# Norms, scaling and gate rows one stage ahead, joins pipelined by token half, shifted norms written in full first

## The reference

```
x = x + 0.5 * swiglu(rmsnorm(x, ffn1_norm[i]), ...)
h = rmsnorm(x, mix_norm[i]);  x = x + mixer(h)       # deltanet, stick-breaking, sparse attention, deltanet
x = x + 0.5 * swiglu(rmsnorm(x, ffn2_norm[i]), ...)
```

```
m = split(silu(c) @ mod_w + mod_b, 9)       # shift, scale, gate for three places
modulate(x, g, shift, scale) = rmsnorm(x, g) * (1 + scale) + shift
x = x + 0.5 * gate * swiglu(modulate(x, ...))
```

## Time and profile before

| | us |
|---|---|
| median of 3 runs | 3886.77 (3882.24 to 3892.0) |
| the profiled execution's own time | 3886.8 |
| its span, first to last instruction | 3885.0 |
| PE busy | 3564.5 (92%) |
| DVE busy | 2276.5 (59%) |
| ACT busy | 1839.1 (47%) |
| POOL busy | 606.9 (16%) |

### The profile page before, as it was taken

How to read it: one execution, slowest core, us unless ns; L and a number is a source line. 1 busy time by engine, 2 the same in 40 slices (tenths; PEclk the granted TensorE clock), 3 DMA queues, 4 the chain that set the end, 5 groups by cost and what they waited for, 6 DMA issues and landing times. The chain is left out here.

```text
span 3885.0 us, 45081 instructions
## 1 busy us (share of the span) xinstructions
PE 3564.5 (92%) x18342; PEld 2997.1 (77%) x18342; DVE 2276.5 (59%) x2608; ACT 1839.1 (47%) x2400; POOL 606.9 (16%) x208
## 2 busy tenths in 40 slices
PE   7998799999899996899998799899998789999999
PEld 6887677788778876688887688787878568787887
DVE  4475458776566667656666454555555554555654
ACT  4453257665356562456554244444443344444443
POOL 0001129572042320142400200000000000000000
PEclk9998899999999998899998899999999899999999
DMA  5542046665276752376743035454544115354453
GB/s 217 188 148 87 1 174 239 225 240 204 101 271 233 275 206 106 134 258 238 265 166 131 1 109 189 153 189 149 198 163 164 62 68 194 142 200 157 152 195 136
DMA packets 89978, 653.57 MB, mean 168 GB/s; under 512 B 10032, under 2 KB 10032, under 8 KB 10928
## 3 DMA queue, kind: packets, MB, share of 16 engines
q1 hardware_dynamic: 78768, 573.10, 40.4%
q0 software_dynamic: 11008, 77.60, 5.6%
HBM read 649.61 MB, written 1.05 MB: 167 GB/s over the span
## 5 line engine op out<-in xcount | busy, mean ns | idle before, releaser
L1424 DVE TENSOR_TENSOR w_lo<-raw,w_hi 128x2048 fp32r<-128x2048 f32 x540 | 1421.0, 2636 | 661.0 <-ACT w_hi L1003 660.7
L1003 ACT ACTIVATE w_hi<-raw 128x2048 fp32r<-128x2048 f32 x540 | 1031.0, 1913 | 601.2 <-PE acc L518 410.2
L516 PE MATMUL wrk<-w_hi,h_hi 128*128 128x512 f32 (+1 forms) x2496 | 973.3, 390 | 61.5 <-DVE w_lo L1424 41.4
L518 PE MATMUL wrk<-w_hi,h_lo 128*128 128x512 f32 (+1 forms) x2496 | 956.2, 383 | 0.0
L517 PE MATMUL wrk<-w_lo,h_hi 128*128 128x512 f32 (+1 forms) x2496 | 955.1, 383 | 0.0
L516 PEld LDWEIGHTS wrk<-w_hi,h_hi 128*128 128x128 f32 x2496 | 473.7, 190 | 157.8 <-DVE w_lo L1424 52.3
L2082 POOL TENSOR_TENSOR arena<-arena,c 128x2048 f32<-128x2048 f32 x92 | 492.1, 5356 | 473.1 <-ACT arena L1003 447.1
L518 PEld LDWEIGHTS wrk<-w_hi,h_lo 128*128 128x128 f32 x2496 | 472.9, 189 | 93.3
L517 PEld LDWEIGHTS wrk<-w_lo,h_hi 128*128 128x128 f32 x2496 | 474.0, 190 | 85.2 <-issue 0.2
L516 PE MATMUL acc<-w_hi,hid_hi 128*128 128x512 f32 x1144 | 447.9, 392 | 9.4 <-DVE hid_lo L1507 9.4
L518 PE MATMUL acc<-w_hi,hid_lo 128*128 128x512 f32 x1144 | 445.9, 390 | 0.0
(11 more groups left out here) (254 smaller groups left out, 3501.4 us busy)
## 6 DMA issues: line engine op xcount, KB each, us to landing
raw<-in_wts SPq DMA_DIRECT2D x540, 1024.0 KB, 4.8
arena<-in_mods POOLq DMA_DIRECT2D x72, 1024.0 KB, 5.2
const<-in_const SPq DMA_DIRECT2D x1, 2176.0 KB, 10.1
c<-in_bias POOLq DMA_DIRECT2D x8, 256.0 KB, 3.4
x<-in_x SPq DMA_DIRECT2D x1, 1024.0 KB, 5.3
c<-in_c SPq DMA_DIRECT2D x1, 1024.0 KB, 4.8
out<-x SPq DMA_DIRECT2D x1, 1024.0 KB, 3.9
row<-in_rows SPq DMA_DIRECT2D x1, 512.0 KB, 11.5
```

Of the source, the lines that this page charges most:

```text
L516: nc.tensor.matmul(o, l_h, r_h, start=first, stop=False, skip_group_check=True)
L518: return nc.tensor.matmul(o, l_l, r_h, start=False, stop=last, skip_group_check=True)
L1003: return nc.scalar.activation(o, i, f, **kw)
L1424: tt(w_lo[:, ns % SLOTS, :], raw[:, ns % SLOTS, :], w_hi[:, ns % SLOTS, :].bitcast(F32), ALU.subtract).then_inc(lo_ready, 1)
```

## The change

`mod` and `final_norm` no longer stand between stages: the silu rows are made in step 1 of ffn2_0, `mod` in step 2 of ffn2_3, the final norm in step 2 of b0_ctx (`INSIDE`). The statistics and the normalise of b0_ctx, b0_ffn0 and b0_attn's context are made in step 4 of the operation before (`AHEAD`), and c is loaded at the start of ffn2_3. `follower` now names the next operation whatever it is. `opens` has three kinds: "ready" (normalised ahead), "late" (as before) and "norm". Ahead of ready and late ones the last FFN turns t=0 between its last downs. Ahead of norm ones the t=0 downs of the last step come before the t=1 downs of the step before it, statistics and normalise of t=0 are done before the last product, and t=0 is turned right behind it. The openings of all kinds are reordered on PE, ACT and DVE. Gate rows move into step 6 of the FFNs of the second network; attention and convolution keep them at their start. With a shift, ACT writes the four scaled and shifted blocks in full to `shifted`, waits for them, and copies them rounded to h_hi in one instruction; DVE subtracts the two in one. `stat` has two sets, for alternate norms.

```diff
+    ops.insert(len(ops) - 1, ("mod", "mod", {}))
+    ops.append(("ffn", "b0_ctx", dict(x="c", l=0, s=0)))
     ops.append(("final", "final_norm", dict(x="x", a="final_norm")))
-    ops.append(("mod", "mod", {}))
-    ops.append(("ffn", "b0_ctx", dict(x="c", l=0, s=0)))
...
+INSIDE = dict(rows="ffn2_0", mod="ffn2_3", final_norm="b0_ctx")
+AHEAD = dict(ffn2_3="b0_ctx", b0_ctx="b0_ffn0", b0_ffn0="b0_attn")
+ROWS_AT, MOD_AT, FINAL_AT, AHEAD_AT, GATE_AT = 1, 2, 2, 4, 6
...
+        def opens(i):
+            if ops[i][1] in AHEAD.values():
+                return "ready"
+            return "late" if late(ops[i][0], ops[i][2]) else "norm"
...
-            sp.wait_ge(x_new, before(first_c, "x"))
+            sp.wait_ge(x_new, before(op_at("ffn2_3"), "x"))
             sp.dma_start(c[:], c_d[:]).then_inc(c_loaded, 16)
...  (PE, turn)
+                    if opens(i) == "ready" and not nth:
+                        last = [k for k in range(i) if ops[k][0] in UPDATES and ops[k][1] not in INSIDE][-1]
+                        _, ready, count = stream(last)
+                        pe.wait_ge(ready, count + 2 * t + half + 1)
...  (PE, ffn)
+                early = nxt and opens(nxt) != "norm"
                 turn(i, 0, 0)
                 turn(i, 0, 1)
+                gate_up(0, 0, 0)
                 turn(i, 1, 0)
-                gate_up(0, 0, 0)
                 turn(i, 1, 1)
+                gate_up(0, 1, 0)
                 gate_up(0, 0, 1)
-                gate_up(0, 1, 0)
                 gate_up(0, 1, 1)
...
                     down(s - 1, 0, 0)
+                    if s == STEPS - 1 and not early:
+                        turn_hid(s)
                     down(s - 1, 0, 1)
                     if s == STEPS - 1:
-                        turn_hid(s)
+                        if early:
+                            turn_hid(s)
+                        else:
+                            down(s, 0, 0)
+                            down(s, 0, 1)
                     down(s - 1, 1, 0)
                     down(s - 1, 1, 1)
+                    if name == "ffn2_0" and s == ROWS_AT:
+                        rows(i, name)
+                    if "l" in prm and s == GATE_AT:
+                        gate_rows(i, name, prm)
...
                 down(STEPS - 1, 1, 1)
+                if nxt and not early:
+                    turn(nxt, 0, 0)
+                    turn(nxt, 0, 1)
...  (ACT, turned_high)
+                    if shift is None:
+                        m = fn(h_hi[:, k, tok(t)], v, ACT.Copy, scale=a)
+                    else:
+                        steps.mark(fn(shifted[:, 8 * t + k, :], v, ACT.Identity, scale=a, bias=shift))
+                if shift is not None:
+                    steps.wait()
+                    m = fn(h_hi[:, 4 * half:4 * half + 4, tok(t)], shifted[:, 8 * t + 4 * half:8 * t + 4 * half + 4, :], ACT.Copy)
...  (ACT, ffn)
+                if mode == "norm":
+                    split_to(ns)
+                    statistics(i, halves=(0,))
                 split_to(ns + 1)
-                if scaled:
-                    turned_high_all(i)
-                    split_to(ns + 2)
-                    statistics(i)
-                else:
-                    statistics(i)
-                    turned_high_all(i)
-                    gate_rows(i, name)
-                    split_to(ns + 2)
+                turned_high(i, 0, 0)
+                turned_high(i, 0, 1)
+                if mode == "norm":
+                    statistics(i, halves=(1,))
+                turned_high(i, 1, 0)
+                turned_high(i, 1, 1)
+                split_to(ns + 2)
+                if mode == "late":
+                    statistics(i)
...  (ACT, ffn, in step s, behind silu_gate)
+                    if "l" in prm and s == GATE_AT:
+                        gate_rows(i, name)
+                    if name == "ffn2_0" and s == ROWS_AT:
+                        rows(i, name)
                     split_to(ns + 3 * s + 3)
                     for g in mine[2:]:
                         modulation(g)
+                    if name == "b0_ctx" and s == FINAL_AT:
+                        nc.scalar.preload_act_table_set("natural_log_exp_and_others")
+                        statistics(op_at("final_norm"))
+                        nc.scalar.preload_act_table_set("silu_and_others")
+                    if name in AHEAD and s == AHEAD_AT:
+                        j = op_at(AHEAD[name])
+                        act.wait_ge(der_ready, 1)
+                        nc.scalar.preload_act_table_set("natural_log_exp_and_others")
+                        statistics(j, src=(c, c_new, before(j, "c")) if ops[j][0] == "attn" else None)
+                        nc.scalar.preload_act_table_set("silu_and_others")
...  (ACT, opening of mixers)
+                split_to(ns)
+                statistics(i, halves=(0,))
                 split_to(ns + 1)
-                statistics(i)
-                turned_high_all(i)
+                turned_high(i, 0, 0)
+                statistics(i, halves=(1,))
+                turned_high(i, 0, 1)
+                turned_high(i, 1, 0)
+                turned_high(i, 1, 1)
...  (DVE, turned_low)
-                if shifts:
-                    steps.wait()
...
+                else:
+                    ks = slice(4 * half, 4 * half + 4)
+                    m = tt(h_lo[:, ks, tok(t)], shifted[:, 8 * t + 4 * half:8 * t + 4 * half + 4, :], h_hi[:, ks, tok(t)].bitcast(F32), ALU.subtract)
...  (DVE, ffn)
+                turned_low(i, 0, 0)
+                turned_low(i, 0, 1)
+                if opens(i) == "norm":
+                    normalise(i)
+                split_to(ns + 1)
+                turned_low(i, 1, 0)
+                turned_low(i, 1, 1)
+                split_to(ns + 2)
...  (DVE, add_out)
-                    if nxt and b >= 2:
-                        turned_low(nxt, 0, b - 2)
+                    if nxt and b >= 2 and opens(nxt) != "norm":
+                        turned_low(nxt, 0, b - 2, prm=prelude_prm(nxt))
+                    if nxt and b == 1 and opens(nxt) == "norm":
+                        normalise(nxt, halves=(0,))
...  (DVE, opening of mixers)
+                split_to(ns)
+                turned_low(i, 0, 0)
                 normalise(i)
-                split_to(ns + 1)
-                turned_low_all(i)
+                turned_low(i, 0, 1)
+                turned_low(i, 1, 0)
+                turned_low(i, 1, 1)
                 split_to(ns + 2)
...  (POOL, modulation)
-                    pool.wait_ge(taken, use["rows", "row3"] + 1)
+                    pool.wait_ge(taken, use[name, "mrow3"] + 1)
```

More of the change, by code:

```diff
@@ L216, in bank_uses @@
     if kind == "ffn":
-        return ["row0", "row1"] * ("l" in prm) + [f"{n}" for s in range(STEPS) for n in (f"gu{s}0", f"gu{s}1", f"t{s}")]
+        rows_at = {GATE_AT: ["row0", "row1"]} if "l" in prm else {ROWS_AT: [f"mrow{r}" for r in range(4)]} if prm["a"] == "ffn2_norm0" else {}
+        return [n for s in range(STEPS) for n in [f"gu{s}0", f"gu{s}1"] + rows_at.get(s, []) + [f"t{s}"]]
     if kind == "final":
         return []
-    if kind == "rows":
-        return ["row0", "row1", "row2", "row3"]
-    if kind == "mod":
+    if kind in ("rows", "mod"):
         return []
@@ L430, in follower, with op_at, stat_of @@
                 j += 1
-            ok = j < len(ops) and late(ops[j][0], ops[j][2]) and all(k not in UPDATES for k, _, _ in ops[i + 1:j])
-            return j if ok and ops[j][2]["x"] == ops[i][2]["x"] else None
+            return j if j < len(ops) else None
+        def opens(i):
+            if ops[i][1] in AHEAD.values():
+                return "ready"
+            return "late" if late(ops[i][0], ops[i][2]) else "norm"
+        def op_at(name):
+            return [k for k, o in enumerate(ops) if o[1] == name][0]
+        def stat_of(i, nth=0):
+            return stat[:, (before(i, "norm") + nth) % 2, :]
         def turned_bank(i, t, half, nth=0):
@@ L491, in _ @@
             first_c = [i for i, o in enumerate(ops) if o[2].get("x") == "c"][0]
-            ahead = starts[first_c]["ns"] + SLOTS - 1
+            ahead = starts[op_at("ffn2_3")]["ns"] + SLOTS
             load_all(0, ahead)
-            sp.wait_ge(x_new, before(first_c, "x"))
+            sp.wait_ge(x_new, before(op_at("ffn2_3"), "x"))
             sp.dma_start(c[:], c_d[:]).then_inc(c_loaded, 16)
@@ L693, in out_proj @@
                 part(3, 0).then_inc(acc_full, 1)
-                if nxt:
+                early = nxt and opens(nxt) != "norm"
+                if early:
                     turn(nxt, 0, 0)
                 part(2, 1).then_inc(w_used, 1)
-                if nxt:
+                if early:
                     turn(nxt, 0, 1)
                 part(3, 1).then_inc(w_used, 1)
+                if nxt and not early:
+                    turn(nxt, 0, 0)
+                    turn(nxt, 0, 1)
             def gdn(i, name, prm):
@@ L992, in _ @@
```

(18 more changed lines are left out.)

101 lines of the change are left out of this document (39 added, 62 removed).

## The result

The changed kernel takes 3838.45 us (median of 4 runs, 3836.41 to 3843.95) against 3885.34 us (4 runs) for the kernel before: ratio 0.9879, 95% interval 0.9865 to 0.9894. The profiled execution took 3836.4 us, its span 3834.6.

A forecast was written before the change was run, and what follows sets the result against it. TensorE (PE), busy 92% of 3885.0 us, was taken as the bound, so only its queue or idle time counts. Terms for the joins summed to 21.7 us off 3886.8, forecast 3865 (3856 to 3874, chance 0.58); range 3848 to 3882.

The forecast's parts named there:

- five terms: FFN joins: gains of 13.0 (b0_ctx), 4.8 (b0_ffn0) and 1.0 us (b1_ffn0); 3.3 lost each in b0_ffn1 and b1_ffn1.
- the silu rows: Join into ffn2_0: 8.3 us won, minus 3.7 inside the stage and a PE stall; 2.0 kept, bounds -3 and 4.6.
- the four mixers with their ends: Mixer openings gain 6.6 us, ends of ffn1_0 to ffn1_3 lose 6.8: together -0.2.
- b0_attn: Context turn made ready ahead gains 6.6 us; its second turn, 9.0 against 10.57, gains 1.5.
- b1_conv: Opening reordered, gate rows unmoved: gain 3.5 us.
- the late joins: Both turns behind gate_up(0,0,0) expose 0.55 to 0.6 us; 12.45 becomes 13.1, six times 0.6, 3.6 lost.
- The rival of the two-step copy: ACT's wait before the Copy makes a bank 3.0 instead of 2.1 us, 14 more: 3879, no measurable change; chance 0.10.
- Stall PE some 2.6: ffn2_0: the w_hi behind ACT's held gates of step 2 and a contended w_lo stall PE some 2.6 us.
- a sign of being wrong: Wrong if steps 4 or 6 show PE waiting for w_lo, or if ffn2_0 takes longer than before.
- The slower rival: POOL's late start in ffn2_0 passes down to job 23: stage ends 24 us later, 11 more, total 3900; chance 0.06.
- The work moved inside: Statistics ahead (5.9 us on ACT) and gate rows at step 6 stay covered; else up to 6 or 2 us per place.
- the rival: Clock: short stalls in new openings keep PE at half clock; seven norm joins lose 1.4 us more each, 3875; chance 0.16.

The follow-up runs named there:

- e8: Kernel before with one part alone: shifted norms evicted in full by ACT and subtracted once by DVE; 3865.56 us, ratio to before 0.9953.
- e6: Changed kernel with a third order of turn_hid(10) and the last downs at the end of a FFN before a norm; 3840.30 us, ratio to before 0.9886.

## Why the prediction was right or wrong

**The step that failed** is the "before" side of five terms: b0_ctx, b0_ffn0, b0_ffn1, b1_ffn0 and b1_ffn1. It took the windows of the earlier trace rows from E to PE's wait for a w_lo and set against them the time to "the first product of step 1". Two gate_ups were missing on one side: 5.5 to 5.6 us for each join beyond the half clock already counted (6.94 - 1.4, 8.24 - 2.7, 5.57, 8.50 - 3.0, 5.56), 27.7 in all. With them the sum is 21.7 + 27.7 = 49.4, and the profiled executions differ by 50.4. The terms of b0_ctx, b0_ffn0 and b1_ffn0 then come within 0.2 us of the table, those of b0_ffn1 and b1_ffn1 within 1. That the whole comes so near is in part luck: the silu rows (4.4 worse than forecast) and the four mixers with their ends (2.8 worse) are made up by b0_attn (2.2 better), b1_conv (1.9), the late joins (1.8) and 2.8 us that had no term. The count of PE's instructions in the same rows would have shown the missing gate_ups. This also turned the sign of b0_ffn1 and b1_ffn1, "3.3 lost", which won 1.7 and 1.9 net.

**The joins after the change** were right within 0.2 us in the FFNs: 12.31 for 12.5, 12.71 for 12.9, 17.58 for 17.6, and the second turn 9.03 for 9.0. The block of eviction takes ACT the 2.1 us that had been assumed:

```profile
2478.80 1.51 ACT L1034 ACTIVATE arena<-acc,der 128x128 f32<-128x128 f32 x4 [1.19 <-PE acc L583]
2480.34 0.63 ACT L1034 ACTIVATE h_hi<-arena 128x512 fp32r<-128x512 f32 x1
```

The rival of the two-step copy (3.0 a bank) is out by these figures, and e8 puts the eviction at 20 us alone. b0_attn's first product came 5.30 after E, not 6.4, which is half of the 2.2 us by which that stage beat its forecast; the other half lies behind its second turn, and its cause is not shown. b1_conv's came at 9.12, not 10.65.

**Mixer openings and ends**: 7.1 to 7.6 to the first product for 7, and 4.7 won in all four for 6.6. The predicted stalls at the ends came: in ffn1_1 2.85 behind 1.09, against "3". Total 7.7 for 6.8. The 1.1 ahead of turn_hid(10), from moving it before its gates were done, had been priced at nothing; e6 shows that it needn't be paid.

```profile
912.66 0.66 PE L627 MATMUL wrk<-const,arena 128*128 128x128 f32 x4 [1.09 <-DVE arena L1552]
...
917.56 0.47 PE L530 MATMUL acc<-w_hi,hid_hi 128*128 128x512 f32 x1 [2.85 <-DVE hid_lo L1558]
```

**The silu rows**: the order of events was as forecast, POOL's second pair 52.7 us after E (50.1 before) and ACT in front of step 2's gates; the size was not. "Stall PE some 2.6" was 7.3, so a gain of 2.0 became a loss of 2.4, which the text had named as a sign of being wrong. The slower rival, a slip down to the last job, did not come.

**Late joins** lost 1.8, not 3.6. In ffn1_1, ffn1_2 and ffn1_3 nothing was lost (13.09, 12.95 and 13.00 us to step 1 against 13.01, 13.13 and 13.12), and PE's wait for w_lo ahead of step 1 in ffn1_1 fell from 1.18 to 0.62 us, so the exposed transposes took the place of a wait there. The 1.8 were lost in ffn2_1 (1.4) and ffn2_3 (0.6).

**The work moved inside** was covered: in steps 4 and 6 PE has no idle time over 0.4 us in b0_ctx and b0_ffn0. Their rests grew by 3.2. The transposes made early are 0.95 of it, by which ffn2_3's rest grew with them alone, and the gate rows 2.2 for a forecast of 1.95.

**The clock** went mostly the other way than the rival had it. The joins of b0_ctx, b0_ffn0 and b1_ffn0 stood at 0.75, 0.80 and 0.81 before and at 1.00 after; all half-clock time in the trace fell from 323 to 280 us. This was already in the sum as 1.4, 2.7 and 3.0. b0_ffn1 and b1_ffn1 fell from 1.00 to 0.90, 1.4 us more of PE as the rival said, but they took 17.58 and 17.56 us like b1_ffn0 at 1.00, where PE had idle time in that place:

```profile
3337.92 1.09 PE L583 MATMUL acc<-const,h 128*128 128x128 f32 x8 [0.62 <-DVE h L1529]
3340.12 0.50 PE L530 MATMUL wrk<-w_hi,h_hi 128*128 128x512 f32 x1 [1.11 <-DVE w_lo L1480]
```

In the other two no such wait is over 0.4 us: the slower work filled them.

The rule of the Trainium skill that was weighed ("TensorE: Matmul & The Clock Gate", "What's actually happening", activity releases the throttle) agrees with the trace in the ready openings, where PE is busy 11.95 of 12.31 us and held 1.00, and decides nothing in the others: with equal instructions two of the norm openings fell to 0.90 and one held 1.00.

## What to carry to other kernels

Before two windows are subtracted, count the instructions of the bounding engine in both: if the counts differ by more than the change explains, they don't end at the same point. Put a join's eviction on the engine that has nothing else queued there, since 1.3 us of DVE for each bank cost up to 5.7 us in a join where the same queue carries the adds and the next weights (the fall of the clock to 0.80 included). And where a kernel's clock dips inside a stage that wasn't edited, judge an edit of a few us by its own stretch of the trace and not by the time of the whole.

## What the runs showed of the hardware

In ffn2_0 DVE and POOL shut each other out by whole instructions. In the rows above POOL's product at 572.65 ends at 577.18, and the w_lo begun at 571.99 ends at 579.35, 2.17 behind it (it began while an earlier product of POOL, 568.11 to 572.70, still ran, and POOL's next one went first); the next w_lo ends at 585.93, and POOL's product begun at 583.75 then needs 4.48 more, to 590.41. Each took its usual time once the other was done. So the 14.0 us of two w_lo hold 4.6 of work. The Trainium skill, "SBUF — State Buffer", "SBUF: two separate sides", says that these two engines take their shared port for a whole instruction (DVE when it has two SBUF inputs, as here) and that the other blocks, and does not share; the trace agrees, with 2.17 and 4.48 us behind the other's end.

Stages with the same instructions differed by up to 6.4 us of 300 (mix_3) and 6.9 of 276 (b0_attn) between the traces, and so did their time at the 1.2 GHz level (54.6 to 71.7 us in mix_3); whether the kernel or the single execution makes the difference is not shown. The FFN joins of the second network, where their code was the same, repeated within 0.1 us (12.31 to 12.36 for b0_ctx in nine traces).
